# A state space stream with its dependent steps moved apart, the norm's roots at its end, and three small DMAs issued earlier

## The chip, the cores and the metric

The kernel runs on one core of one Trainium2 chip. The metric is device time in microseconds (us) of one execution, the median of several. TensorE (PE) multiplies, VectorE (DVE), ScalarE (ACT) and GpSimd (POOL) do the elementwise work, SyncE (SP) issues the weights' DMAs.

## The reference

Two blocks over 272 tokens (16 meta tokens and 256), width 1024. The first has layer norms, SwiGLU, a short convolution and a forgetting attention. The second, where the change is, has one mixer and one convolutional FFN. Of the mixer, this matters:

```python
u = rmsnorm(h, norm_w)
z, xbc, dt_raw, q, k, v, g_ssd, g_att = split_cols(u @ w_in, IN_WIDTHS)
xbc = silu(causal_dwconv(xbc, conv_w, conv_b))             # 4 taps
xs, bm, cm = split_cols(xbc, (2048, 512, 512))
dt = softplus(dt_raw + dt_bias) * valid
cs = cumsum(dt * a)
# 32 heads of 64, 8 heads share one of 4 groups of B and C:
lmat = exp(where(causal, cs[l] - cs[s], -inf))
y = einsum(C @ B^T, lmat, xs * dt) + d_skip * xs
g = y * silu(z)                                            # gated_group_rmsnorm
g = g * rsqrt(mean(g * g over each of 4 groups of 512) + EPS) * ssd_norm_w
y_ssd = g @ w_ssd_branch
merged = sigmoid(g_ssd + gb0) * y_ssd + sigmoid(g_att + gb1) * y_att
h = h + merged @ w_out
```

## The kernel before

**Weights.** Every product with a weight is done in three matmuls of float32r: the weight is split into a high half `wh` (ScalarE, a rounded copy, `high`) and a low half `wl` (VectorE or, for pieces named in `P.pool`, GpSimd, `low` and `low_pool`), and TensorE adds high by high, low by high and high by low (`gemm`, L834 and L836). A group is 256 output columns and, for 1024 rows, one unit of weights: 1 MB, one DMA on SP's queue, 4 pieces, 48 matmuls. A unit is split three groups ahead, in four pieces spread over the group that runs. Two pairs of PSUM banks alternate between groups.

**Side work.** All other work of the attention, the norms and the stream is cut into steps, one generator for each engine (`pe_steps`, `act_steps`, `dve_steps`, `pool_steps`). `Plan` says after which matmul of which group the next step is taken: `queue(n)` makes n steps available, `rate` is how many are taken in a group, `drain` takes what is left. All engines take the same number of steps at the same points of the groups, each in its own instruction order; a step may be empty (a bare `yield`, `idle(n)`). What an engine waits for is told by semaphores alone, and an engine that waits holds up all that stands behind it.

**The stream.** The conv output xs comes in 8 groups `("xs", j)` of two 128-row chunks, c = 2j and 2j+1; each chunk is two heads, h = 2c and 2c+1. `conv4` (taps) puts a group into CY: ScalarE the first tap, VectorE the other three for both chunks. `act_conv_end` makes TH = tanh(CY/2), `dve_conv_end` CY = (TH+1)*CY. Then, for each c, in this order of steps: y of c-2 (`pe_ssd_y`, products of XDT and EX; `dve_ssd_y` writes YB, adding the skip; `pool_ssd_y` multiplies by ZS, silu of z); the transposes of CY (L767) to PS[6], which VectorE scales by dt into XDT; a step for each head, in which TensorE broadcasts the cumulative sums (CSH, CSL) to PS[4] or PS[5], VectorE (even head) or ScalarE (odd head, two Relu passes) makes the exponent's argument, ScalarE the Exp, GpSimd the product with CBM, C B^T masked. Four EX buffers hold two c. Pair j ran in the group after xs j, its conv end as its first step.

**The norm.** After y of each fourth chunk, `act_gn`, `dve_gn` and `pe_gn` did a whole group g in five steps: squares of four chunks into SY (L1068), VectorE's sum of two halves (L1680), TensorE's mean (L670, L671) into PS[6], Ln and Exp on ScalarE (`act_rstd`, L953 and L955), the scale of YB (L1685), the high halves YH (L1079) and the low halves YL (L1691). Ln and Exp stand in another table set than the one the stream's Exp and Tanh use, so each norm group loads two tables.

**Behind the stream** come the groups `("gs", j)`, 4 of 258 columns, over which the last steps run, and `("ys", j)`, two units each, which read YH and YL.

**Ahead of it**, at the start of the mixer, GpSimd's queue issues eight small DMAs (L2092 to L2100): sinks, four cuts of the bias strips (2.2 MB in all, B2, B1, B0), and `ssd_dt_bias`, `ssd_a_log`, `ssd_d` (semaphore s_d). ScalarE waits for the last three before the scaled copy DC (L1344), and behind that stand the splits of the next unit and ZD (L1348), which empties the PSUM bank of the group dt. Softplus and a cumulative sum in nine dependent VectorE steps (L1471) follow ZD, then its transposes (L729).

Of the kernel before, what the change touches and what calls it, by code (L numbers as in the profile page):

```python
# [13 lines left out]
T = 272  # L14
# [169 lines left out]
def build(nc, A, out, scratch, ctx):  # L184
# [103 lines left out]
    with ExitStack() as st:  # L288
# [6 lines left out]
        SY = sb(st, "SY", [128, 4, NV])  # L295
# [43 lines left out]
    s_gsq, s_gadd, s_gsum, s_gn, s_yh, s_yl = (sem(n) for n in ("gsq", "gadd", "gsum", "gn", "yh", "yl"))  # L339
    s_gs2, s_gsg, s_m1, s_m2 = sem("gs2"), sem("gsg"), sem("m1"), sem("m2")  # L340
# [126 lines left out]
    def ssd_steps(c):  # L467
        return 3 + (c > 1) + 5 * (c > 1 and (c - 2) % 4 == 3)
    P.credit, P.rate, P.pool = -1.0, 8, (2,)
    for j in range(8):  # L470
# [4 lines left out]
        P.queue(1 + ssd_steps(2 * j) + ssd_steps(2 * j + 1))  # L475
    P.queue(7)
# [188 lines left out]
    def pe_gn(e, g):  # L665

        yield
        e.wait_ge(s_gadd, g + 1)
        e.wait_ge(s_xd, min(16, 4 * g + 5))
        e.matmul(PS[6][:, 0:NV], mean5[:], SY[:, 0, :], start=True, stop=False)  # L670
        e.matmul(PS[6][:, 0:NV], mean5[:], SY[:, 1, :], start=False, stop=True).then_inc(s_gsum, 1)  # L671
        yield
        yield from idle(3)

    def pe_steps(e):
# [73 lines left out]
        yield  # L749
        for c in range(16):  # L750
            if c % 2 == 0:
                yield
            if c > 1:
                pe_ssd_y(e, c - 2)
                yield
                if (c - 2) % 4 == 3:
                    yield from pe_gn(e, (c - 2) // 4)
# [5 lines left out]
            if c > 4 and (c - 5) % 4 == 0:  # L763
                e.wait_ge(s_lnv, 8 + (c - 5) // 4)
# [4 lines left out]
            yield  # L769
            for h in (2 * c, 2 * c + 1):  # L770
# [12 lines left out]
        for c in (14, 15):  # L783
            pe_ssd_y(e, c)
            yield
        yield from pe_gn(e, 3)
# [276 lines left out]
    def act_gn(e, g):  # L1063

        e.wait_ge(s_yz, 4 * g + 4)
        if g:
            e.wait_ge(s_gsum, g)
        e.activation(SY[:], YB[:, 4 * g:4 * g + 4, :], ACT.Square).then_inc(s_gsq, 1)  # L1068
        yield
        yield  # L1070
        e.wait_ge(s_gsum, g + 1)
        if g:
            e.wait_ge(s_gn, g)
        act_rstd(e, PS[6][:, 0:NV], 1, NV, 7 + g)
        yield
        e.wait_ge(s_gn, g + 1)
        for k0 in (4 * g, 4 * g + 2):
            for k in (k0, k0 + 1):
                e.activation(YH[:, k, :], YB[:, k, :], ACT.Copy, scale=pc("ssd_norm_w_2", k)).then_inc(s_yh, 1)  # L1079
            yield  # L1080

    def act_steps(e):
# [65 lines left out]
        yield from idle(5)  # L1148
        for c in range(16):
            if c % 2 == 0:  # L1150
                act_conv_end(e, 4 + c // 2)
                yield
# [801 lines left out]
    def pool_steps(e):  # L1954
# [30 lines left out]
        for c in range(16):  # L1985
            if c % 2 == 0:
                yield
# [187 lines left out]
```

## Time and profile before

| | us |
|---|---|
| median of 3 runs | 1780.92 (1780.73 to 1780.99) |
| the profiled execution, its own time | 1781.4 |
| its span | 1779.6 |
| TensorE busy | 1665.9 (94%) |
| VectorE busy | 1021.5 (57%) |
| ScalarE busy | 931.1 (52%) |
| GpSimd busy | 211.3 (12%) |

A share of the span is a mean over stages with different limits: the projections of the FFNs run with TensorE hardly ever idle, and the two stages in which it stops are read by themselves below. "Busy" of TensorE says nothing about its clock: the granted clock is a column of its own. In the waits, a row says which engine waited at which line for which instruction of another engine.

### The profile page before, as it was taken

To read this page: it belongs to the slowest core of one execution; us is meant where nothing else is said; L and a number is where in the kernel's file an instruction comes from. 1 tells how busy PE (TensorE), PEld (TensorE's weight loads), DVE (VectorE), ACT (ScalarE), POOL (GpSimd) and SP (SyncE) were. 2 spreads that over 40 slices of the span, in tenths; PEclk is the share of its full clock that TensorE was granted. 3 is DMA by queue.
4 is the path that set the end of the run, shared out by engine and by line. 5 is a ranking of instruction groups with operands and counts; after the bars stand their busy time and mean duration, and the time that the engine had idled before them with its cause. 6 is when DMAs were issued, how large, how long until landed. Compare 5 with 4: busy or idle time off the path is not lost. (4 is left out here: it accounts for less than half of the span.)

```text
span 1779.6 us, 31457 instructions
## 1 busy us (share of the span) xinstructions
PE 1665.9 (94%) x12901; PEld 1597.4 (90%) x12901; DVE 1021.5 (57%) x2083; ACT 931.1 (52%) x2018; POOL 211.3 (12%) x224
## 2 busy tenths in 40 slices
PE   8999999999999999999899997799997669999998
PEld 7999989899997999998899996788987558999997
DVE  6555566655545655554565554545375655668862
ACT  5444454644436544465554434566755556456652
POOL 4000000000000000001000001255423332200000
PEclk9999999999999999999999998999998889999999
DMA  8555535355554555553356553533442114545551
GB/s 258 184 167 172 184 123 186 119 181 175 171 172 131 178 179 179 159 160 101 119 167 190 178 181 102 151 102 112 134 151 62 58 48 126 182 143 190 183 165 56
DMA packets 260207, 266.00 MB, mean 149 GB/s; under 512 B 4755, under 2 KB 259025, under 8 KB 260064
## 3 DMA queue, kind: packets, MB, share of 16 engines
q1 hardware_dynamic: 258528, 260.72, 46.5%
q0 software_dynamic: 1536, 3.28, 0.8%
q8 instruction: 102, 1.67, 0.4%
q14 instruction: 41, 0.34, 0.1%
HBM read 262.89 MB, written 1.09 MB: 148 GB/s over the span
## 5 line engine op out<-in xcount | busy, mean ns | idle before, releaser
L1708 DVE TENSOR_TENSOR wl<-raw,wh 128x512 fp32r<-128x512 f32 x925 | 608.4, 711 | 392.4 <-ACT wh L1199 384.8
L1199 ACT ACTIVATE wh<-raw 128x512 fp32r<-128x512 f32 (+1 forms) x989 | 550.2, 621 | 213.0 <-PE ps L834 212.2
L834 PE MATMUL ps<-XH,wh 128*128 128x272 f32 (+2 forms) x2264 | 584.1, 293 | 21.4 <-ACT ZD L1348 8.6
L836 PE MATMUL ps<-XH,wl 128*128 128x272 f32 (+2 forms) x2264 | 574.4, 289 | 0.0
L834 PEld LDWEIGHTS ps<-XH,wh 128*128 128x128 f32 x2264 | 435.6, 192 | 27.1 <-issue 14.7
L836 PEld LDWEIGHTS ps<-XH,wl 128*128 128x128 f32 x2264 | 436.9, 193 | 0.2
L834 PE MATMUL ps<-XL,wh 128*128 128x272 f32 (+2 forms) x2264 | 319.1, 290 | 0.3 <-DVE XL L1463 0.3
L834 PEld LDWEIGHTS ps<-XL,wh 128*128 128x128 f32 x2264 | 294.8, 191 | 7.0 <-DVE XL L1463 4.2
L834 PE MATMUL ps<-HH,wh 128*128 128x272 f32 (+1 forms) x704 | 173.1, 284 | 0.0
L836 PE MATMUL ps<-HH,wl 128*128 128x272 f32 (+1 forms) x704 | 173.1, 284 | 0.0
L834 PEld LDWEIGHTS ps<-HH,wh 128*128 128x128 f32 x704 | 132.5, 188 | 0.0
L836 PEld LDWEIGHTS ps<-HH,wl 128*128 128x128 f32 x704 | 132.4, 188 | 0.0
L834 PE MATMUL ps<-KXH,wh 128*128 128x256 f32 (+1 forms) x480 | 121.2, 291 | 2.3 <-ACT KXH L943 2.3
L836 PE MATMUL ps<-KXH,wl 128*128 128x256 f32 (+1 forms) x480 | 118.0, 284 | 0.0
L1239 ACT ACTIVATE HH<-SG 128x272 fp32r<-128x272 f32 (+1 forms) x88 | 33.7, 426 | 148.4 <-DVE SG L1725 148.4
L2032 POOL TENSOR_TENSOR wl<-raw,wh 128x512 fp32r<-128x512 f32 x64 | 86.1, 1350 | 158.9 <-ACT wh L1199 158.9
L834 PEld LDWEIGHTS ps<-KXH,wh 128*128 128x128 f32 x480 | 91.2, 190 | 7.0 <-issue 5.4
L834 PE MATMUL ps<-HL,wh 128*128 128x272 f32 (+1 forms) x704 | 93.6, 284 | 0.0
L836 PEld LDWEIGHTS ps<-KXH,wl 128*128 128x128 f32 x480 | 91.5, 191 | 0.1
L834 PEld LDWEIGHTS ps<-HL,wh 128*128 128x128 f32 x704 | 89.0, 188 | 0.0
L1234 ACT ACTIVATE SG<-ps 128x272 f32<-128x272 f32 (+1 forms) x88 | 29.7, 389 | 102.8 <-PE ps L834 102.7
L1725 DVE SCALAR_TENSOR_TENSOR SG<-SG,ps 128x272 f32<-128x272 f32 (+1 forms) x88 | 33.8, 426 | 82.0 <-PE ps L834 82.0
(376 smaller groups left out, 1991.0 us busy)
## 6 DMA issues: line engine op xcount, KB each, us to landing
raw<-in_ffn_wg SPq DMA_DIRECT2D x44, 1024.0 KB, 5.4
raw<-in_ffn_wu SPq DMA_DIRECT2D x44, 1024.0 KB, 5.4
raw<-in_w_in SPq DMA_DIRECT2D x33, 1024.0 KB, 5.3
raw<-in_ffn_wd SPq DMA_DIRECT2D x32, 1024.0 KB, 5.1
raw<-in_w_ffn_in SPq DMA_DIRECT2D x22, 1024.0 KB, 5.1
raw<-in_ffn_wd SPq DMA_DIRECT2D x16, 768.0 KB, 4.7
raw<-in_conv_w_in SPq DMA_DIRECT2D x12, 1024.0 KB, 5.1
raw<-in_kv_w SPq DMA_DIRECT2D x8, 1024.0 KB, 5.4
```

Source lines behind the costliest of these rows:

```text
L834: mm = e.matmul(o, hi[:, k, c], xk, start=u.first and part == 0 and k == 0, stop=u.last and end)
L836: e.matmul(o, lo[:, k, c], xk, start=False, stop=False)
L1199: e.activation(wh[u.n % NH][:, c], raw[u.n % NR][:, c], ACT.Copy).then_inc(s_hi, 1)
L1234: e.activation(sg[:, m, n0:T], PS[G.b0 + m][:, 0:T - n0], ACT.Silu).then_inc(s_sg, 1)
L1239: e.activation(HH[f][:, 2 * j + m, n0:T], sg[:, m, n0:T], ACT.Copy).then_inc(s_hh, 1)
L1708: e.tensor_tensor(wl[u.n % NR][:, c], raw[u.n % NR][:, c], wh[u.n % NH][:, c].bitcast(F32), ALU.subtract).then_inc(s_lo, 1)
L1725: e.scalar_tensor_tensor(out=sg[:, m, n0:T], in0=sg[:, m, n0:T], scalar=0.5, in1=PS[G.b0 + m][:, 0:T - n0], op0=ALU.mult, op1=ALU.mult).th ...
L2032: e.tensor_tensor(wl[u.n % NR][:, c], raw[u.n % NR][:, c], wh[u.n % NH][:, c].bitcast(F32), ALU.subtract).then_inc(s_lop, 1)
```

## The change

1. **Order of the stream.** Pair j runs one group later, in the group after xs j+1. The conv end of the next group is taken between the two chunks of a pair (after the first transposes for ScalarE, after the argument for VectorE) instead of directly ahead of its own transposes. In each c one step does both heads on ScalarE, in the order Relu, Relu (odd), Exp (even), Exp (odd), and both products on GpSimd.
2. **Norm.** Squares, sum and mean of group g are taken in three different c (6+4g, 7+4g, 8+4g) and the mean is copied to a new tile VS. Ln and Exp of groups 0 to 2 are done at once, over 774 columns, at the end; group 3's after its own mean. The scales and the halves of all four groups follow there.
3. **Tables.** The set loaded ahead of the BC groups is `exp_and_others` instead of `natural_log_exp_and_others`; that one is loaded at the stream's end.
4. **Plan.** Other counts of steps, and a rate of 12 instead of 11.5 in the gs groups.
5. **Small DMAs.** The three of s_d are issued ahead of the sinks and the strips.

```diff
     def ssd_steps(c):
-        return 3 + (c > 1) + 5 * (c > 1 and (c - 2) % 4 == 3)
+        return 3 + (c > 1) + 2 * (c % 2 == 0 and c < 14) + (c > 5 and (c - 6) % 4 < 3)
...
             P.credit, P.rate = -4.0, 11.5
-        P.queue(1 + ssd_steps(2 * j) + ssd_steps(2 * j + 1))
-    P.queue(7)
+            P.queue(2)
+        else:
+            P.queue(ssd_steps(2 * j - 2) + ssd_steps(2 * j - 1))
+    P.queue(ssd_steps(14) + ssd_steps(15) + 12)
+    P.rate = 12
...
     def pe_gn(e, g):
-        yield
         e.wait_ge(s_gadd, g + 1)
-        e.wait_ge(s_xd, min(16, 4 * g + 5))
+        e.wait_ge(s_xd, (9, 13, 16, 16)[g])
+        if g:
+            e.wait_ge(s_vs, g)
...
-            if c > 4 and (c - 5) % 4 == 0:
-                e.wait_ge(s_lnv, 8 + (c - 5) // 4)
+            if c in (9, 13):
+                e.wait_ge(s_vs, (c - 5) // 4)
...
+        if step == 2:
+            e.wait_ge(s_gsum, g + 1)
+            e.activation(VS[:, g, :], PS[6][:, 0:NV], ACT.Copy).then_inc(s_vs, 1)
+
+    def act_gn_root(e, g0, g1):
+        e.wait_ge(s_vs, g1)
+        e.activation(VS[:, g0:g1, :], VS[:, g0:g1, :], ACT.Ln, bias=cc[:, 1:2]).then_inc(s_gl, 1)
+        e.wait_ge(s_gl, 1 if g0 == 0 else 2)
+        e.activation(VS[:, g0:g1, :], VS[:, g0:g1, :], ACT.Exp, scale=-0.5).then_inc(s_gr, 1)
...
+            if c % 2 == 0 and c < 14:
+                act_conv_end(e, 5 + c // 2)
                 yield
-        yield from idle(2)
-        yield from act_gn(e, 3)
+            yield
+            h = 2 * c + 1
+            E = EX[h % 4]
...
+            e.wait_ge(s_e, c + 1)
+            e.activation(EX[(h - 1) % 4][:], EX[(h - 1) % 4][:], ACT.Exp).then_inc(s_ee, 1)
+            e.wait_ge(s_er, c + 1)
+            e.activation(E[:], E[:], ACT.Exp, scale=-1.0).then_inc(s_ee, 1)
...
+        act_gn(e, 2, 2)
+        yield
+        e.preload_act_table_set("natural_log_exp_and_others")
+        yield
+        act_gn_root(e, 0, 3)
+        yield
+        yield
+        act_gn(e, 3, 0)
+        yield
+        act_gn_high(e, 0)
...
-        e.preload_act_table_set("natural_log_exp_and_others")
+        e.preload_act_table_set("exp_and_others")
...
+        dve_ssd_y(e, 15)
+        yield
+        dve_gn_scale(e, 0)
+        yield
+        dve_gn_low(e, 0)
+        yield
+        dve_gn_scale(e, 1)
+        dve_gn_add(e, 3)
+        yield
+        dve_gn_low(e, 1)
...
+        dd = A["ssd_d_2"]
+        e.dma_start(DTB[:], A["ssd_dt_bias_2"].rearrange("l p -> p l")).then_inc(s_d, 16)
+        e.dma_start(AN[:], A["ssd_a_log_2"].rearrange("l p -> p l")).then_inc(s_d, 16)
+        e.dma_start(DC2[:], bass.AP(tensor=dd.tensor, offset=dd.offset, ap=[[0, 128], [1, 32]])).then_inc(s_d, 16)
         e.dma_start(SNK[:], bass.AP(tensor=sk.tensor, offset=sk.offset, ap=[[0, 128], [1, 16]])).then_inc(s_b, 16)
```

VectorE in the stream before, one projection group: after the taps (CY from PSUM) one split, then the conv product (CY from TH), and at once YB, XDT and the argument of the next chunk.

```order
L1766 SCALAR_TENSOR_TENSOR CY<-ps,PV,CY 128x269 x2
L1708 TENSOR_TENSOR wl<-raw,wh 128x512
L1675 SCALAR_TENSOR_TENSOR CY<-TH,CY 128x272 x2
L1708 TENSOR_TENSOR wl<-raw,wh 128x512
L1699 SCALAR_TENSOR_TENSOR YB<-CY,DC,ps 128x258
L1649 TENSOR_TENSOR XDT<-ps,DTT 128x256
L1651 TENSOR_TENSOR XDT<-ps,DTT 16x128
L1661 TENSOR_SCALAR EX<-ps,NCT 128x272
L1662 TENSOR_SCALAR EX<-ps,NCT 128x144
```

And after the change, the same place, here with a norm group's sum (SY) in it:

```order
L1829 SCALAR_TENSOR_TENSOR CY<-ps,PV,CY 128x269 x2
L1771 TENSOR_TENSOR wl<-raw,wh 128x512
L1744 TENSOR_TENSOR SY<-SY 128x516
L1762 SCALAR_TENSOR_TENSOR YB<-CY,DC,ps 128x258
L1771 TENSOR_TENSOR wl<-raw,wh 128x512
L1686 TENSOR_TENSOR XDT<-ps,DTT 128x256
L1688 TENSOR_TENSOR XDT<-ps,DTT 16x128
L1699 TENSOR_SCALAR EX<-ps,NCT 128x272
L1700 TENSOR_SCALAR EX<-ps,NCT 128x144
L1739 SCALAR_TENSOR_TENSOR CY<-TH,CY 128x272 x2
```

The conv product (CY from TH) moved from ahead of XDT to behind the first chunk's argument: it now serves the pair that follows.

VectorE at the end of the stream after the change, from y of chunk 15 on (scale: YB from VS; low halves: YL):

```order
L1762 SCALAR_TENSOR_TENSOR YB<-CY,DC,ps 128x258
L1771 TENSOR_TENSOR wl<-raw,wh 128x512
L1749 TENSOR_TENSOR YB<-YB,VS 128x1032
L1755 SCALAR_TENSOR_TENSOR YL<-YB,PV,YH 128x258 x4
L1749 TENSOR_TENSOR YB<-YB,VS 128x1032
L1744 TENSOR_TENSOR SY<-SY 128x516
L1755 SCALAR_TENSOR_TENSOR YL<-YB,PV,YH 128x258 x4
```

The sum of the last norm group's squares (SY) stands behind the scale and low halves of group 0 and the scale of group 1.

## Rows read from the trace of the kernel before

**Rows 1.** Windows: length, busy PE PEld DVE ACT POOL, clock, DMA share, GB/s.
```profile
1328.50:1498.40 169.90, 123.22 (x849) 109.32 (x848) 97.88 (x201) 91.37 (x182) 60.80 (x60) 0.85 0.22 69
```

**Rows 2.** Waits, 1320 to 1500 us: total us, times, longest us.
```profile
PE ps L767 <- DVE CY L1675: 30.5, 8, 6.9
...
PE ps L670 <- DVE SY L1680: 13.9, 4, 4.5
```

**Rows 3.** Timeline of TensorE from 1409 us: start us, length, what [idle before].
```profile
1409.50 1.16 PE L670 MATMUL ps<-SY,mean 128*128 128x258 f32 x2 [4.47 <-DVE SY L1680]
...
1410.96 3.05 PE L834 MATMUL ps<-XL,wh 128*128 128x272 f32 x14
...
1414.22 0.29 PE L836 MATMUL ps<-XH,wl 128*128 128x272 f32 x1
...
1414.81 0.29 PE L836 MATMUL ps<-XH,wl 128*128 128x272 f32 x1
...
1417.07 0.29 PE L836 MATMUL ps<-XH,wl 128*128 128x272 f32 x1
...
1418.59 0.29 PE L836 MATMUL ps<-XH,wl 128*128 128x272 f32 x1
```

**Rows 4.** Timeline of TensorE from 1123 us, a run of 16 matmuls.
```profile
1128.65 2.17 PE L834 MATMUL ps<-XL,wh 128*128 128x272 f32 x16
```

**Rows 5.** Timeline of TensorE from 1474 us: first matmuls of gs 3 and ys 0.
```profile
1492.77 0.28 PE L834 MATMUL ps<-XH,wh 128*128 128x258 f32 x1
...
1498.53 0.28 PE L834 MATMUL ps<-YH,wh 128*128 128x258 f32 x1
```

**Rows 6.** Groups by line, 1330 to 1490 us: count, busy us, mean ns, idle.
```profile
L1997 POOL TENSOR_TENSOR EX<-EX,CBM 128x416 f32<-128x416 f32 x32 | 34.3, 1072 | 70.3 <-ACT EX L1171 63.6 <-ACT EX L1168 6.7
...
L1708 DVE TENSOR_TENSOR wl<-raw,wh 128x512 fp32r<-128x512 f32 x28 | 24.3, 871 | 17.6 <-ACT wh L1199 17.6
...
L1675 DVE SCALAR_TENSOR_TENSOR CY<-TH,CY 128x272 f32<-128x272 f32 x16 | 8.2, 555 | 1.2 <-ACT TH L1061 1.2
```

**Rows 7.** DMA issues from 1100 to 1130 us: KB each, us to landing.
```profile
SNK<-in_attn_sinks POOLq DMA_DIRECT2D x1, 8.0 KB, 2.9
...
DC<-in_ssd_d POOLq DMA_DIRECT2D x1, 16.0 KB, 12.7
```

**Rows 8.** Timelines of ScalarE and TensorE from 1100 us, two waits and the transposes.
```profile
1119.45 0.45 ACT L1344 ACTIVATE DC<-DC 64x16 f32<-64x16 f32 x2 [14.45 <-DMA DC<-in_ssd_d]
...
1123.10 0.60 PE L834 MATMUL ps<-XH,wh 128*128 128x272 f32 x1 [8.56 <-ACT ZD L1348]
...
1136.81 0.21 PE L729 MATMUL ps<-ident,ZD 32*128 32x32 f32 x1 [0.98 <-issue]
```

**Rows 9.** Timeline of VectorE from 1350 us: the taps of one group.
```profile
1358.14 2.60 DVE L1766 SCALAR_TENSOR_TENSOR CY<-ps,PV,CY 128x271 f32<-128x271 f32 x6 [0.54 <-ACT CY L1253]
```

**Rows 10.** The page's groups, whole kernel: the splits on VectorE.
```profile
L1708 DVE TENSOR_TENSOR wl<-raw,wh 128x512 fp32r<-128x512 f32 x925 | 608.4, 711 | 392.4 <-ACT wh L1199 384.8
```

**Rows 11.** Timeline of ScalarE from 1326 us: squares and a root's table load.
```profile
1369.49 1.06 ACT L1068 ACTIVATE SY<-YB 128x1032 f32<-128x1032 f32 x1 [2.38 <-POOL YB L2024]
...
1373.29 1.28 ACT L955 ACT_TABLE_LOAD   x1
```

**Rows 12.** Timeline of VectorE from 1350 us: a scale, four low halves.
```profile
1375.04 1.23 DVE L1685 TENSOR_TENSOR YB<-YB,RS 128x1032 f32<-128x1032 f32 x1 [3.15 <-ACT RS L955]
...
1376.85 1.70 DVE L1691 SCALAR_TENSOR_TENSOR YL<-YB,PV,YH 128x258 fp32r<-128x258 f32 x4 [0.58 <-ACT YH L1079]
```

**Rows 13.** Instructions on the tile raw, the window 1103 to 1104: unit z 0.
```profile
L2144 SPq DMA_DIRECT2D raw<-in_w_in x1: 368/368/368, 1103.5 to 1103.5; - x1
...
DMA to landing us min/median/max: 17.2/17.2/17.2
```

**Rows 14.** Timeline of VectorE from 1119 us: first split of z 0, last sum.
```profile
1127.39 0.69 DVE L1708 TENSOR_TENSOR wl<-raw,wh 128x512 fp32r<-128x512 f32 x1
...
1136.29 0.42 DVE L1471 TENSOR_TENSOR CSB<-CSB 32x272 f32<-32x272 f32 x1
```

More of the change, by code:

```diff
@@ L749, in pe_steps @@
         yield
+        yield from idle(2)
         for c in range(16):
-            if c % 2 == 0:
-                yield
             if c > 1:
@@ L769, in pe_steps @@
             yield
+            yield from idle(c % 2 == 0 and c < 14)
             for h in (2 * c, 2 * c + 1):
@@ L782, in pe_steps @@
                 yield
[L783 to L786, printed above, removed]
+            yield from idle(c % 2 == 0 and c < 14)
+            if c > 5 and (c - 6) % 4 < 3:
+                if (c - 6) % 4 == 2:
+                    pe_gn(e, (c - 6) // 4)
+                yield
+        pe_gn(e, 2)
+        yield
+        pe_ssd_y(e, 14)
+        yield
+        yield
+        pe_ssd_y(e, 15)
+        yield
+        yield from idle(3)
+        pe_gn(e, 3)
+        yield
+        yield from idle(4)
         for j in range(4):
@@ new lines, in act_steps @@
+            e.wait_ge(s_e, c + 1)
[3 more added lines that the diff above has]
+            yield
+            yield from idle(c % 2 == 0 and c < 14)
+            if c > 5 and (c - 6) % 4 < 3:
+                act_gn(e, (c - 6) // 4, (c - 6) % 4)
+                yield
+        act_gn(e, 2, 2)
+        yield
+        e.preload_act_table_set("natural_log_exp_and_others")
@@ L1655, in dve_steps @@
             yield
+            yield from idle(c % 2 == 0 and c < 14)
             h = 2 * c
@@ L1928, in vector @@
         side.run(at["out2"])
-        norm(11, UT2, 8, TS, "norm_ffn_w_2", 64)
+        norm(7, UT2, 8, TS, "norm_ffn_w_2", 64)
         for j in range(11):
@@ L1984, in pool_steps @@
         yield
+        yield from idle(2)
         for c in range(16):
-            if c % 2 == 0:
-                yield
             if c > 1:
@@ L1990, in pool_steps @@
                 yield
-                if (c - 2) % 4 == 3:
-                    yield from idle(5)
+            yield
+            yield from idle(c % 2 == 0 and c < 14)
             yield
@@ L1997, in pool_steps @@
                 e.tensor_tensor(E[:], E[:], CBM[:, g, 0:416], ALU.mult).then_inc(s_em, 1)
-                yield
-        for c in (14, 15):
-            pool_ssd_y(e, c)
             yield
-        yield from idle(5 + 4)
+            yield from idle((c % 2 == 0 and c < 14) + (c > 5 and (c - 6) % 4 < 3))
+        yield
+        pool_ssd_y(e, 14)
+        yield
+        yield
+        pool_ssd_y(e, 15)
+        yield
+        yield from idle(8 + 4)
         for k in range(KD):
```

142 lines of the change are left out of this document (73 added, 69 removed).

## The prediction

> **What bounds the kernel now.** I read the groups of instructions first: TensorE is busy 94% of the span, so time is lost only where it stops or runs at its lower clock. The waits, cut to one stage after the other, show two such places.
>
> The first is the state space stream, from the end of the projection group xs 0 (1328.5 us) to the first matmul on YH (1498.4 us), 169.9 us. TensorE is busy 123.2 us of them at a mean granted clock of 0.85 [rows 1]. The waits name the idle 46.7 us: 30.5 us in 8 waits of the transposes of CY for VectorE's half of the convolution's end, 13.9 us in 4 waits of the norm's mean for VectorE's sum of squares [rows 2]. Each long wait has a tail: after the 4.47 us wait at 1409.5 the matmuls of about 0.21 us (14 from 1410.96 on, 3.05 us) are those of the lower level of the clock, 1.2 GHz [rows 3].
>
> What would the stage take with no wait at 2.4 GHz? A projection matmul of 272 columns takes (2.17 - 0.29) / 15 = 0.125 us [rows 4], a group of 48 takes 6.03 us; a group of 258 columns takes 1498.53 - 1492.77 = 5.76 us [rows 5]. Seven xs groups and four gs groups: 42.2 + 23.0 = 65.2 us. One step c of the stream adds its transposes (1414.22 to 1414.81, less two matmuls: 0.34 us), four broadcasts at 0.125 (0.50 us) and the y products (1417.07 to 1418.59, less two matmuls: 1.27 us) [rows 3]: 2.11 us, 16 times, 33.8 us. Four norm means cost 1409.50 to 1410.96 = 1.5 us at half clock, about 0.85 at full: 3.4 us. The floor is 102.4 us, so 67.5 us of the stage are loss: 46.7 us idle and 20.8 us of slow clock.
>
> The second place is at 1114.5 us. ScalarE waits for a small table (ssd_d) until 1119.45, 14.45 us, TensorE 8.56 us behind it [rows 8]. ssd_d took 12.7 us to land because it was issued behind the bias strips; the sinks table, issued ahead of them, took 2.9 us [rows 7]. After the stall TensorE runs at the lower level for 3.1 us, the first matmul taking 0.60 us [rows 8]: about 1.5 us more.
>
> **The stream, part by part.** The work of TensorE is the same, 538 projection matmuls from the last BC product to YH in both orders; only positions change. Before, a pair of steps c ran in the group after its projection: 12 matmuls and one y product after that group's end its transposes came, while ScalarE and VectorE still had to do the taps (2.60 us on VectorE after ScalarE's first tap [rows 9]), the tanh and the product. Now the pair runs one group later and its convolution end is half a group before its first transposes. For xs 1: projection ends, taps done about 3.2 us later, tanh at 3.9, product by about 7.0 where VectorE has a scale step in front of it; the transposes come 60 matmuls and two steps' other work (1.7 us) after, at 9.2 us. Eight waits, 30.5 us, go.
>
> What is late next? In the steady part TensorE needs 6.03 + 4.22 = 10.25 us for a pair. I followed VectorE in the new order from a projection's end: taps to 3.2 us, split, YB 4.2, split, XDT 5.4, exponent argument 6.2, conv product 7.0, YB 7.4, XDT 8.05, split, argument 9.4 (with 0.48 for a YB, 0.42 + 0.27 for XDT and 0.49 + 0.35 for an argument, the means of the groups by line). TensorE asks for YB at 5.85, XDT at 7.2, the argument at 7.95: about 1.7 us of cover each. The y products of c need two GpSimd products of 1.07 us [rows 6]; they are done about 3 us before. This exchange of ScalarE's Relu and Exp costs nothing at that cover; without it each c would pay.
>
> VectorE is nearly full, though. Its 97.9 us in this stage [rows 1] are nearly unchanged in content against a floor of 102.4. Part of them is stretching: the 28 splits took 871 ns on average here against 711 over the whole kernel, and the 16 conv products 555 ns against an undisturbed 430 or so, 28 x 0.16 + 16 x 0.125 = 6.5 us [rows 6, 10]. GpSimd's 60.8 us come closer together in a stage of 113 us, so I take half as much again, 3 us, and 1 us for the start of the stream, where two steps stand close: **4 us** of new stall together (bounds 0 and 20 us, rival 1).
>
> The rule behind that is the Trainium skill's, page "SBUF — State Buffer", section "Who interferes with whom": a VectorE instruction with two SBUF inputs and a GpSimd instruction that reads SBUF exclude one another for the whole instruction. It speaks against packing this stage tighter. The taps, which read one input from PSUM, show no such stretching here (493 ns on average, 487 least), so the trace agrees.
>
> **The norm.** For groups 0 to 2 the squares, the sum, the mean and a copy to VS are a step c apart (5 us), so their three waits in the stream go. The mean of group 2 comes where c = 15 is dense: squares at ScalarE after its exponentials, VectorE's sum behind a split: 0.8 us late. All roots go to the end: 8 table loads of 1.28 us [rows 11] leave ScalarE, one is added, and the first load of the stream too goes, since the set that is loaded ahead now holds tanh. ScalarE was not what TensorE waited for, so I count that at nothing.
>
> The Trainium skill's page "ScalarE: Activation LUTs", section "What ACT_TABLE_LOAD costs", has about 2.66 us for a switch with its drain; here the Exp follows its load at once, so the row's 1.28 us decides. By either figure TensorE's sum stays as it is, as ScalarE has slack.
>
> The last mean pays for this. From the end of y 15: root of groups 0 to 2 ready at about +1.1 us (copy, load, two takes of GS, a split, Ln and Exp over 774 columns); VectorE then does a whole scale of group 0 (1.23 us), four low halves (1.70 us) that wait for ScalarE's high halves, which stand behind the squares of group 3 (1.06 us) [rows 11, 12], and the scale of group 1, before it sums group 3's squares. That ends at about +6.4 us; TensorE gets there at +1.9: **4.5 us** of stall, and 1.6 us of slow clock after it, as at 1409.5. Behind it stand 72 matmuls, 8.6 us; ScalarE's last high halves are needed only in the second unit of the first ys group, 6 us later still. They are ready at about +15 us, so ys starts on time.
>
> Stage: 102.4 + 4 + 0.8 + 4.5 + 1.6 = 113.3 us, against 169.9: **56.6 us less**.
>
> **The small DMAs.** Moved ahead of five others, three issues of 0.53 us: the strips start 1.7 us later. Their first reader stands behind four more projection groups, so that costs nothing. ssd_d lands about 2.9 us after its issue, by 1105.5, where ScalarE gets to it. TensorE passes 1114.5 without its 8.56 us. What is late next is a weight load: unit z 0, issued at 1103.5, took 17.2 us [rows 13] beside the strips, to 1120.7. VectorE's first split of it was at 1127.39 before, and its cumulative sums, in order behind it, ended at 1136.71, 9.3 us later [rows 14]; TensorE's transposes that need them came at 1136.81 [rows 8]. Now the split can start at 1121.4, the sums end at 1130.7, and TensorE, there by 1125.5, stops for 5 us. The rest of the kernel moves by 6.0 us; the new stop is long enough to lower the clock, 1.5 us. **4.5 us less.** Bounds: 3.2 if the strips hold z 0 back by another 1.3 us, 7.5 if the weights, with a head start, land 1.5 us earlier and the clock holds.
>
> **The sum.** The profiled execution took 1781.4 us with a span of 1779.6, 0.5 us above the median of 1780.92. 1781.4 - 56.6 - 4.5 = 1720.3; against the median 1719.8. I say **1720 us**.
>
> **The rivals.**
> 1. VectorE becomes the bound. For: 98 us of work in 102. If each of five two-input instructions of a pair waits for half a GpSimd product (0.55 us) instead of 0.17, a pair costs 1.9 us more on VectorE, over eight pairs 15 us. Against: margins of 1.7 us take up part. **1735 us.**
> 2. The convolution's end is not early enough, since each engine takes it in order behind other steps. If half of the 30.5 us stays (at other instructions perhaps) with half of the clock's loss, 15 + 10 us: **1745 us.**
> 3. Slower than before: GpSimd's pair of products reaches TensorE too late in every step c. ScalarE now starts Relu before it has VectorE's argument and does both Exp behind it. It decides from 3 us of lateness on, my cover; each microsecond more costs 16. To eat 60 us the chain of two products (2.1 us) and three ScalarE passes would have to come 6.8 us later than I have it. The rows show GpSimd idle for 70.3 us ahead of these products, waiting for ScalarE's Exp [rows 6], which speaks for the mechanism, and TensorE never waiting for the products, which speaks against it. A new lateness of 7 us: **1784 us.**
> 4. The order doesn't do what it says. The instruction rows above show that it does: no separate chance.
>
> **How the numbers follow.** Forecast 0.62, rival 1 0.22, rival 2 0.13, rival 3 0.03. The forecast's own bounds are 1710 (no new stall from packing, the clock kept twice, 7.5 us from the DMAs) and 1730; with rival 1 and its neighbourhood to 1743 the range holds more than 8 in 10: **1710 to 1743**. A measurement tells 0.2%, 3.6 us, from no change. Faster by more: 0.96; within: 0.01; slower: 0.03.
>
> **What would show it.** In the profile of the changed kernel: no wait of the CY transposes for the conv product over 1 us; mean waits of groups 0 and 1 at zero and one wait of 4 to 5 us before the last; granted clock 1.00 from the third xs group to the second gs group; the wait for ssd_d gone and TensorE idle about 5 us before the transposes of ZD; stage near 113 us; splits in it at 0.9 to 1.0 us. It is wrong if pairs take over 11.5 us each, or if TensorE waits for YB or XDT in each step.

## The result and the profile after

The changed kernel takes **1731.55 us** (median of four; 1726.82 to 1734.70) against 1780.83 for the kernel before: ratio 0.9722, 95% interval 0.9699 to 0.9745. That is 49.3 us less, where I had forecast 61 less and 1720; the time lies inside the range. The kernel before kept within 1 us in these four runs (within 3 to 4 us over nine runs in each later measurement), the changed one spread over 8 us, and that needs an explanation of its own.

The profiled execution is the 1734.70 one, span 1732.9. The same stretch as in [rows 1], from the end of xs 0 to the first matmul on YH; columns: stretch, length, busy time and count of PE, PEld, DVE, ACT and POOL, granted clock, DMA share, GB/s. The second row is all that follows it:

```profile
1324.20:1451.70 127.50, 111.01 (x851) 97.90 (x850) 100.56 (x200) 80.90 (x175) 68.19 (x60) 0.92 0.29 92
...
1452.00:1732.90 280.90, 267.88 (x2203) 265.73 (x2202) 184.54 (x352) 155.37 (x314) 17.12 (x15) 0.98 0.48 154
```

The stage fell from 169.9 to 127.5 us: 42.4 less, forecast 56.6 less. TensorE is idle 16.5 us of it (46.7 before); 127.5 - 16.5 - 102.4 leaves 8.6 us of slow clock (20.8 before). Behind YH nothing changed: 281.2 us to the span's end, as before. What TensorE waited for in the stage (us in total, times, longest), against [rows 2]:

```profile
PE ps L675 <- DVE SY L1744: 10.0, 2, 6.2
PE ps L675 <- DVE XDT L1688: 3.4, 1, 3.4
PE ps L675 <- issue: 1.9, 1, 1.9
PE ps L664 <- DVE YB L1762: 0.9, 2, 0.7
PE ps L781 <- DVE EX L1700: 0.2, 1, 0.2
```

The eight waits of the CY transposes (30.5 us) are gone, and nearly nothing stands in the steps themselves. All that is left, 15.3 us, is L675: the four means of the norm, 3.4, 1.9, 3.8 and 6.2 us. Here are the first and the last of them with what VectorE did ahead of each (start, length, instruction, idle before it and what ended it); first group 0:

```profile
1374.74 2.59 DVE L1829 SCALAR_TENSOR_TENSOR CY<-ps,PV,CY 128x271 f32<-128x271 f32 x6 [1.52 <-ACT CY L1292]
1377.25 0.68 DVE L1771 TENSOR_TENSOR wl<-raw,wh 128x512 fp32r<-128x512 f32 x1
1377.85 0.69 DVE L1744 TENSOR_TENSOR SY<-SY 128x516 f32<-128x516 f32 x1
1378.46 0.47 DVE L1762 SCALAR_TENSOR_TENSOR YB<-CY,DC,ps 128x258 f32<-128x258 f32 x1
1378.85 0.68 DVE L1771 TENSOR_TENSOR wl<-raw,wh 128x512 fp32r<-128x512 f32 x1
1379.45 0.41 DVE L1686 TENSOR_TENSOR XDT<-ps,DTT 128x256 f32<-128x256 f32 x1
1379.79 0.27 DVE L1688 TENSOR_TENSOR XDT<-ps,DTT 16x128 f32<-16x128 f32 x1
...
1380.20 1.20 PE L675 MATMUL ps<-SY,mean 128*128 128x258 f32 x2 [3.41 <-DVE XDT L1688]
```

The mean writes the PSUM bank in which the transposes of CY lie, so it must wait until XDT of step 8 has read them, and VectorE does that XDT behind the taps of the next projection group, 2.59 us, and four other instructions. I had called these waits zero because the sum of squares would be ready. TensorE asks at 1376.8; the sum is there at 1378.5 and the bank at 1380.1, so of the 3.4 us the sum accounts for the first 1.7 and the bank for the rest. For group 1 (asked at 1404.1, sum at 1404.4, bank at 1405.9) nearly all is the bank. Group 3:

```profile
1434.30 1.23 DVE L1749 TENSOR_TENSOR YB<-YB,VS 128x1032 f32<-128x1032 f32 x1
1436.10 1.69 DVE L1755 SCALAR_TENSOR_TENSOR YL<-YB,PV,YH 128x258 fp32r<-128x258 f32 x4 [0.58 <-ACT YH L1096]
1437.70 1.23 DVE L1749 TENSOR_TENSOR YB<-YB,VS 128x1032 f32<-128x1032 f32 x1
1438.85 1.76 DVE L1744 TENSOR_TENSOR SY<-SY 128x516 f32<-128x516 f32 x1
...
1440.66 1.23 PE L675 MATMUL ps<-SY,mean 128*128 128x258 f32 x2 [6.19 <-DVE SY L1744]
```

This is the stall that I forecast, scale, low halves, scale, sum, with 4.5 us; it took 6.2, the sum alone 1.76 us where an undisturbed one takes 0.69. Each of the four stops has slow matmuls behind it: the mean's own two took 1.20 and 1.23 us in these rows. At group 2, whose stop was 3.8 us, they still took 0.70, and the granted clock fell right behind them, to 0.50 in the window from 1428 to 1430.

In the other stretch, that of the small tables, ScalarE no longer waits for ssd_d, and TensorE's wait of 8.56 us [rows 8] is gone. The stop that I had forecast ahead of the transposes of ZD is there, and so is the unit of weights that ScalarE waits for:

```profile
1125.57 1.67 ACT L1238 ACTIVATE wh<-raw 128x512 fp32r<-128x512 f32 x3 [4.49 <-DMA raw<-in_w_in]
...
1129.87 0.28 PE L732 MATMUL ps<-ident,ZD 32*128 32x32 f32 x1 [4.37 <-issue]
```

Sliding window attention starts at 1142.3 instead of 1146.5: 4.2 us gained, forecast 4.5.

### The profile page after: what moved, and what is told of

The parts are those of the page before. It is cut to its first block, busy times and chain, and to the rows that moved or that the text cites. A ratio compares the mean times of both kernels' runs of the same rounds, so it can differ in the third digit from the quotient of the medians.

```text
span 1732.9 us, 31446 instructions
## 1 busy us (share of the span) xinstructions
PE 1654.6 (95%) x12901; PEld 1585.6 (91%) x12901; DVE 1025.5 (59%) x2083; ACT 918.3 (53%) x2010; POOL 219.2 (13%) x224
## 4 chain that ended last, share of the span: by engine, by line
PE 87%; DVE 6%; ACT 5%; issue 2%; DMA 0%; SPq 0%; DVEq 0%; ACTq 0%
PE ps L847 53%; PE ps L849 25%; PE ps L531 1%; DVE wl L1771 1%; ACT wh L1238 1%; DVE CY L1829 1%; ACT XH L956 1%; PE ps L816 1%; PE ps L630 1%; ACT H L961 1%; DVE CY L1739 0%; PE ps L631 0%; PE ps L664 0%; PE ps L619 0%; ACT swP L987 0%
## 5 line engine op out<-in xcount | busy, mean ns | idle before, releaser
L847 PE MATMUL ps<-XH,wh 128*128 128x272 f32 (+2 forms) x2264 | 578.1, 291 | 12.8 <-ACT XH L956 6.7
L849 PEld LDWEIGHTS ps<-XH,wl 128*128 128x128 f32 x2264 | 432.5, 191 | 0.2
```

Source lines behind the costliest of these rows:

```text
L847: mm = e.matmul(o, hi[:, k, c], xk, start=u.first and part == 0 and k == 0, stop=u.last and end)
L849: e.matmul(o, lo[:, k, c], xk, start=False, stop=False)
```

## The experiments

Twelve runs. Times are medians of four or five; the stage runs from the end of xs 0 to the first matmul on YH in the profiled execution, and swa is the start of sliding window attention in it, at which all that comes ahead has been paid.

| kernel | us (lowest to highest) | ratio to before, 95% | swa | stage | TensorE idle in it | clock |
|---|---|---|---|---|---|---|
| before | 1779.4 to 1780.8 (medians) | 1 | 1146.5 | 169.9 | 46.7 | 0.85 |
| changed | 1731.6 (1726.8 to 1734.7) | 0.9699 to 0.9745 | 1142.3 | 127.5 | 16.5 | 0.92 |
| again | 1726.7 (1726.3 to 1730.8) | 0.9698 to 0.9725 | 1136.7 | 124.8 | 16.4 | 0.95 |
| dma_back | 1736.8 (1736.3 to 1738.7) | 0.9748 to 0.9775 | 1148.1 | 125.9 | 16.5 | 0.93 |
| sum3_first | 1726.3 (1725.8 to 1728.9) | 0.9690 to 0.9717 | 1136.8 | 122.8 | 15.8 | 0.96 |
| means_later | 1728.1 (1722.7 to 1729.8) | 0.9691 to 0.9720 | 1142.4 | 121.1 | 14.1 | 0.96 |
| strips_later | 1734.3 (1726.3 to 1734.9) | 0.9710 to 0.9747 | 1141.8 | 127.7 | 16.4 | 0.92 |
| strips_wait | 1727.4 (1725.3 to 1728.5) | 0.9690 to 0.9716 | 1137.1 | 126.5 | 16.4 | 0.93 |
| vector_splits | 1732.0 (1729.2 to 1736.0) | 0.9713 to 0.9739 | 1143.3 | 128.0 | 16.7 | 0.92 |
| short_products | 1723.2 (1723.1 to 1730.5) | 0.9675 to 0.9709 | 1136.9 | 121.3 | 13.0 | 0.94 |
| exp_order | 1739.7 (1739.4 to 1744.5) | 0.9762 to 0.9789 | 1137.0 | 137.2 | 23.2 | 0.90 |
| before_exchange | 1772.9 (1771.9 to 1773.6) | 0.9948 to 0.9973 | 1145.5 | 162.4 | 39.9 | 0.86 |
| best | 1716.8 (1716.1 to 1722.5) | 0.9634 to 0.9662 | 1143.4 | 114.4 | 8.7 | 0.99 |
| best2 | 1718.4 (1717.0 to 1719.1) | 0.9641 to 0.9667 | 1136.8 | 115.4 | 9.4 | 0.99 |

**The changed kernel again.**

> The changed kernel once more, five rounds, to know its spread, since its first four times lay 8 us apart (1726.8 to 1734.7) where the kernel before kept within 1 us. If the spread comes from stops of 3 to 6 us before the norm's means, behind which TensorE falls to 1.2 GHz for a phase that differs from run to run, the times again lie between 1726 and 1735. If it was the chip of that call, they lie within 2 us.

Three of five at 1726.3 to 1726.7, two at 1728.9 and 1730.8; with the first four, four times near 1726.5 and five between 1729 and 1735. The two profiles (1734.7 and 1726.3) say where such runs part, first at a place ahead of everything the diff touches. A norm makes TensorE stop for 6.2 us until 1087 in both, and its matmuls behind that stop run at half clock in both. The clock is back by 1093, then TensorE stops again, for 2.2 us, for the high half of the normed activations (XH). In the 1734.7 run, then in this one:

```profile
1086.00:1092.00 6.00, 5.12 (x11) 3.87 (x12) 0.00 (x0) 2.65 (x5) 0.00 (x0) 0.50 0.00 0
1092.00:1094.00 2.00, 1.38 (x6) 0.81 (x4) 0.00 (x0) 0.55 (x2) 0.00 (x0) 0.97 0.00 0
1094.00:1098.00 4.00, 2.39 (x10) 2.42 (x11) 3.53 (x10) 3.42 (x9) 0.00 (x0) 0.69 0.00 0
```
```profile
1086.00:1092.00 6.00, 5.67 (x15) 4.43 (x16) 0.00 (x0) 2.13 (x4) 0.00 (x0) 0.59 0.00 0
1092.00:1094.00 2.00, 0.49 (x3) 0.06 (x1) 0.42 (x2) 0.92 (x2) 0.00 (x0) 1.00 0.00 0
1094.00:1098.00 4.00, 3.28 (x26) 3.31 (x27) 4.00 (x12) 3.95 (x10) 0.00 (x0) 1.00 0.00 0
```

Behind the stop of 2.2 us the clock falls a second time in the first run, until 1098.9, and holds in this one. Why it does so is not shown. From there it is the DMAs: the release of a weight buffer lets SyncE issue unit z 0 at 1103.4 in the one and at 1101.0 in the other, GpSimd's strips (2.2 MB) start at 1103.2 and 1102.3, and unit z 1, issued at 1108.5 and 1109.1, stands behind them. Issues of that moment (KB, us to landing), first and second run:

```profile
raw<-in_w_in SPq DMA_DIRECT2D x1, 1024.0 KB, 17.1
```
```profile
raw<-in_w_in SPq DMA_DIRECT2D x1, 1024.0 KB, 11.5
```

z 1 lands at 1125.6 or at 1120.6. ScalarE wants it at 1121.1 in the first run and at 1122.7 in the second, so only the first one stops, and loses 5.6 us by the start of sliding window attention. All nine profiled runs that have the new DMA order and do not make the strips wait for z 1 fall on one of these two courses: the clock held behind the 2.2 us in four (again, sum3_first, short_products, exp_order), whose attention starts at 1136.7 to 1137.0, and fell in five (changed, means_later, strips_later, vector_splits, best), where it starts at 1141.8 to 1143.4.

The clock parts the runs once more: this run's stage is 2.7 us shorter at the same idle time, clock 0.95 against 0.92. The first matmuls of the mean of group 1 show where, behind a stop of the same length in both, first and second run:

```profile
1405.98 1.05 PE L675 MATMUL ps<-SY,mean 128*128 128x258 f32 x2 [1.93 <-issue]
```
```profile
1399.33 0.67 PE L675 MATMUL ps<-SY,mean 128*128 128x258 f32 x2 [1.94 <-issue]
```

**The DMA order undone.**

```
         e.dma_start(B0[:], shifted(...)).then_inc(s_b, 16)
+        (dt_bias, a_log, ssd_d again here, behind the sinks and strips)
```

> The changed kernel with the three small loads (dt_bias, a_log, ssd_d) again behind the sinks, the strips and their pieces; the stream stays as changed. Theory: this part alone is worth 4.2 us, the gain read at the first matmul of the sliding window attention (1146.5 before, 1142.3 after), so 1735 to 1737 us, with ScalarE's wait of 14 us for ssd_d and TensorE's 8.6 us back and the 4.4 us before the transposes of ZD gone. Rival: what TensorE gains there is given back, since a later stop moves the clock's low phase, and the time stays within 2 us of the changed kernel's.

1736.8 us: the part is worth about 5 us against the slower course (1731.5) and 10 against the faster one (1726.7). Theory held for the first; I had no term for the second. With the table behind the strips TensorE stops for 9.5 us, until 1124.6 in the profiled run, and all four times lie within 2.4 us. In this order the stop takes up the difference between the courses: before_exchange below, with the old order, is on the fast course, and its attention starts only 1.0 us ahead of the kernel before, which is on the slow one. The change took away the stop that hid the fork.

**The strips later.**

```
-        (four strips issues)
         group("kv2")
         group("dt")
+        group(("q2", 0))
+        (four strips issues)
```

> The changed kernel, with GpSimd's four issues of the strips (2.2 MB) moved from before the group kv2 to behind the group q2 0, some 16 us later. Theory: the changed kernel has two ways through this place. Where TensorE's clock recovers late from the norm before it, weight unit z 1 is issued at 1108.4 beside the strips and lands after 17.1 us, ScalarE waits 4.5 us for it and TensorE 4.4 us with a slow clock behind; where the clock recovers early, it lands after 11.5 us and nothing waits, and the run is 5 us shorter. With the strips out of its way z 1 lands after 6 to 9 us in every run, and all runs lie near the lower value: 1724 to 1728 us, with sliding window attention starting at or before 1137. Rival: the strips now land behind 1137, and VectorE's first sum with them waits: 1730 us or more. Second rival, the strips aren't the cause: the runs again lie in two groups 5 us apart.

This missed its aim. GpSimd has no split in these groups, so its next instruction is still the issue: nothing moved in time, and z 1 took 16.1 us. The run is one more of the changed kernel, 1734.2 to 1734.9 three times and 1726.3 once. The second attempt makes GpSimd wait for z 1:

```
+        z1 = groups["z", 1].units[0].n
+        e.wait_ge(s_raw[z1 % NR], 16 * (z1 // NR + 1))
         (four strips issues)
```

> The changed kernel, with GpSimd waiting for the landing of weight unit z 1 before it issues the strips; the run before this one had moved the issues only past groups in which GpSimd has no work, so the strips still went out at the same time. Theory: z 1 is issued at 1108.4 and, with only z 0 beside it, lands after 5 to 7 us instead of 17.1 (late clock) or 11.5 (early clock). TensorE's wait of 4.4 us before the transposes of ZD and the half clock behind it go, and the two groups of times that the changed kernel shows (1726.5 and 1731.5) close to one: 1723 to 1727. The strips then land by about 1130, ahead of VectorE's first use at 1137. Rival: the strips come too late for that use, or z 2 and z 3 beside them do, 1730 us or more. Second rival: nothing to do with the strips, two groups again.

The strips go out at 1114.7, and z 1, issued at 1109, has landed by then:

```profile
raw<-in_w_in SPq DMA_DIRECT2D x1, 1024.0 KB, 5.3
```

and TensorE's wait ahead of the transposes of ZD is

```profile
1127.35 0.21 PE L732 MATMUL ps<-ident,ZD 32*128 32x32 f32 x1 [1.22 <-issue]
```

The stop fell from 4.4 to 1.2 us, sliding window attention starts at 1137.1 though the clock fell a second time here, and five runs lie within 3.2 us. The strips beside z 1 were what turned the clock's 3 us into the gap of 5.6 us. The repair removes the slower course and gives nothing against the faster one: 1727.4 us against 1726.7.

**The last sum first.**

```
+        dve_gn_add(e, 3)
         dve_gn_scale(e, 0)
...
         dve_gn_scale(e, 1)
-        dve_gn_add(e, 3)
```

> The changed kernel, but VectorE sums the squares of group 3 before it scales group 0, where it stood behind the scale of 0, the low halves of 0 and the scale of 1. Theory: TensorE asks for the last mean at 1434.3 and ScalarE's squares of group 3 end at 1434.8, so the sum ends at 1435.6 and the wait of 6.2 us falls to 1.3 us; with the slow matmuls behind it (about 2 us) 6 to 7 us less than the changed kernel, 1724 to 1726 us. The high and low halves come 0.7 us later and hide. Rival: VectorE is full, and the wait comes back before the first YH matmul: same time as the changed kernel.

1726.3 us, the same as the changed kernel again (1726.7): the stage is 2.0 us shorter, what follows it 2.0 us longer. The wait fell as expected, 6.2 to 1.2 us, and 4.3 us of it came back at the first YH matmul:

```profile
1440.79 0.64 ACT L1262 ACTIVATE GS<-ps 128x258 f32<-128x258 f32 x2
...
1441.52 0.55 PE L847 MATMUL ps<-YH,wh 128*128 128x258 f32 x1 [4.29 <-ACT GS L1262]
```

The rival was right in its result, though what the trace shows is a chain and not VectorE's load. From the first scale to the last high half VectorE and ScalarE pass the four groups to and fro, scale 1.23, high 0.6 until the first low, four lows 1.69: 3.5 us a group, 14 us in a chain, and ScalarE's take of the last GS, which frees the bank that YH needs, stands behind the last high halves. The stall of 6.2 us had covered that chain. The new stop's slow clock falls behind the first YH matmul, which is the 2.0 us: the 56.5 us from there on, in the changed kernel again and here,

```profile
1443.46:1500.00 56.54, 56.07 (x465) 55.76 (x464) 37.84 (x58) 31.83 (x61) 13.30 (x10) 1.00 0.56 187
```
```profile
1441.52:1498.06 56.54, 56.54 (x455) 56.54 (x456) 37.15 (x57) 32.54 (x63) 13.76 (x10) 0.96 0.48 158
```

**The first two means later.**

```
-    (c > 5 and (c - 6) % 4 < 3)          squares, sum, mean in c = 6, 7, 8 and 10, 11, 12
+    (c in NORM)                          in c = 7, 8, 9 and 11, 12, 13; group 2 unchanged
```

> The changed kernel, but squares, sum and mean of groups 0 and 1 each one step c later (7, 8, 9 and 11, 12, 13 for 6, 7, 8 and 10, 11, 12), so that the mean stands behind the XDT of an odd step, which no taps precede on VectorE. Theory: the waits of 3.4 us at 1380 and 1.9 us at 1406 are for XDT of step 8 and 12, which VectorE does behind the taps of the next group; both go, with the slow clock behind them (1.5 to 3 us): 6 to 8 us less, 1723 to 1726 us. Rival, VectorE full: the same 5 us come back as waits of y products or broadcasts, and the time stays within 2 us of the changed kernel's.

Partly. The stage is 121.1 us, 3.7 to 6.4 less, but the waits only fell from 3.4 and 1.9 to 2.7 and 0.8 us, and 2.0 us came back at the y products, which now wait 2.9 us for YB instead of 0.9. The time, 1728.1 us, can't be told from the changed kernel's 1731.6 and 1726.7. VectorE is still behind at the odd step: from the start of the taps it works without a gap for 11 us (1376.3 to 1387.6 in the trace of best).

**What GpSimd's accesses cost.**

```
-                e.tensor_tensor(E[:], E[:], CBM[:, g, 0:416], ALU.mult)
+                e.tensor_tensor(E[:, 0:32], E[:, 0:32], CBM[:, g, 0:32], ALU.mult)
```

> The changed kernel, but GpSimd multiplies only 32 of the 416 columns of each exponential by C-B (32 products of 1.20 us become short; the rest of the product is left out). It measures what GpSimd's accesses cost VectorE. Theory, contention: VectorE's pair of convolution products, 2.2 us where it meets them, falls to 0.9; the sums for the norm from 1.2 and 1.6 to 0.7; the splits from 0.81 to 0.7; so XDT and the sums end 1 to 2 us earlier, the waits before the means of groups 0 and 1 fall from 3.4 and 1.9 us to under 2 together, and the stage from 126 to 129 us to 120 to 122. The wait of 6.2 us before the last mean stays at 5.5 or more, since it is VectorE's order and not its speed. Rival, order alone: the waits of groups 0 and 1 stay over 4 us together and the stage within 2 us.

VectorE's convolution products over the stage (busy, mean ns), changed kernel and this one:

```profile
L1739 DVE SCALAR_TENSOR_TENSOR CY<-TH,CY 128x272 f32<-128x272 f32 x16 | 14.9, 972 | 0.0
```
```profile
L1739 DVE SCALAR_TENSOR_TENSOR CY<-TH,CY 128x272 f32<-128x272 f32 x16 | 10.0, 662 | 0.0
```

So the stretching is real, 555 ns before the change [rows 6], 972 after, 662 without the long products. Against the changed kernel again TensorE's idle time fell by 3.4 us, the stage by 3.5 to 121.3 and the time by 3.5; the first three means wait 2.7, 1.4 and 2.6 us, the last still 6.1. The long products account for a sixth of what the four means wait (15.1 to 12.8 us). GpSimd's splits and its part of y are still there, so a sixth is the least that contention costs; that all the rest is order is not shown. The expected fall to under 2 us together for the first two did not come (4.1).

**More work for VectorE.**

```
-    P.credit, P.rate, P.pool = -1.0, 8, (2,)
+    P.credit, P.rate, P.pool = -1.0, 8, ()
```

> The changed kernel, but VectorE also does the weight splits that GpSimd does in the stream, 11 of 1.37 us on GpSimd, some 0.7 to 0.8 us each on VectorE. It asks whether VectorE is the bound of the stream (my rival 1). If it is, its 8 to 9 us more come out whole, less what GpSimd's 15 us of fewer accesses give back in stretching (2 to 4 us): 4 to 7 us slower than the changed kernel, with new waits of TensorE at y products and broadcasts. If it has slack outside the places before the means, only the two longest waits grow: within 2 us of the changed kernel (1726 to 1732).

1732.0 us. The times can't tell (1729.2 to 1736.0 against 1726.3 to 1734.9 for strips_later beside it); the stage can, 128.0 against 127.5 at the same clock. In the stage VectorE did eight more instructions and GpSimd eight fewer, and VectorE's busy time fell from 100.6 to 97.0 us, since without GpSimd's splits the convolution products took

```profile
L1739 DVE SCALAR_TENSOR_TENSOR CY<-TH,CY 128x272 f32<-128x272 f32 x16 | 7.1, 480 | 0.0
```

7.8 us less than in the changed kernel, more than the splits cost. VectorE's pair of products and then, from GpSimd's timeline, what ran beside it, changed kernel and this one:

```profile
1356.96 2.25 DVE L1739 SCALAR_TENSOR_TENSOR CY<-TH,CY 128x272 f32<-128x272 f32 x2
...
1356.38 1.28 POOL L2098 TENSOR_TENSOR wl<-raw,wh 128x512 fp32r<-128x512 f32 x1
1357.69 2.48 POOL L2059 TENSOR_TENSOR EX<-EX,CBM 128x416 f32<-128x416 f32 x2
```
```profile
1360.68 0.77 DVE L1739 SCALAR_TENSOR_TENSOR CY<-TH,CY 128x272 f32<-128x272 f32 x2
...
1360.82 3.11 POOL L2059 TENSOR_TENSOR EX<-EX,CBM 128x416 f32<-128x416 f32 x2 [1.26 <-ACT EX L1184]
```

Where GpSimd is already at work VectorE's pair takes 2.25 us; where VectorE starts first it takes 0.77 and GpSimd's pair takes 3.11 instead of 2.48. The loss did not go away, it moved to the engine that has time. Because VectorE's busy time fell, this run did not load it harder; what it shows is that 3.6 us less on VectorE do not shorten the stage. That VectorE isn't the bound of the steady part shows in the changed kernel itself: TensorE's groups from 1338.6, 1348.8 and 1359.3 on take 10.2, 10.5 and 11.1 us, with 0.9 us of waits in all, against 10.25 for its own work.

**ScalarE's order in a step.**

```
-            (Relu, Relu of the odd head) (Exp even) (Exp odd)
+            (Exp even) (Relu, Relu of the odd head) (Exp odd)
```

> The changed kernel with ScalarE's order inside a step c as before: Exp of the even head (which waits for VectorE's argument), then the two Relu and the Exp of the odd head; nothing else. My prediction said that without the exchange each c would pay. In the trace of the changed kernel ScalarE's Relus (0.49 and 0.37 us) lie in its wait of 1.4 us for the argument; behind the Exp they make the odd head's Exp 0.9 us later. If each c pays this: 10 to 14 us slower, near 1740 us, with waits of y products for GpSimd's product. If the cover of some 3 us that GpSimd's products had in my sum is real, the exchange is worth nothing: within 2 us of the changed kernel.

1739.7 us, stage 137.2 against 124.8 at the same swa start: 12.4 us. It is not paid at GpSimd's products, nor in each c. VectorE's taps of two successive groups, first in the changed kernel, then here:

```profile
1351.65 2.58 DVE L1829 SCALAR_TENSOR_TENSOR CY<-ps,PV,CY 128x271 f32<-128x271 f32 x6 [1.52 <-ACT CY L1292]
1362.94 2.59 DVE L1829 SCALAR_TENSOR_TENSOR CY<-ps,PV,CY 128x271 f32<-128x271 f32 x6 [1.52 <-ACT CY L1292]
```
```profile
1348.38 2.59 DVE L1829 SCALAR_TENSOR_TENSOR CY<-ps,PV,CY 128x271 f32<-128x271 f32 x6 [2.31 <-ACT CY L1292]
1360.47 2.59 DVE L1829 SCALAR_TENSOR_TENSOR CY<-ps,PV,CY 128x271 f32<-128x271 f32 x6 [2.32 <-ACT CY L1292]
```

ScalarE makes the first tap, right behind the exponentials. With the Relus behind the first Exp it comes 0.8 us later, VectorE waits 2.3 instead of 1.5 us and all that follows in the pair shifts: 12.1 us a pair instead of 11.3. TensorE now waits 1.4 us for YB in two pairs (0.2 and 0.7 before), and the first three means wait 4.8, 3.5 and 5.1 us: 6.8 us of idle time and 5.6 of slow clock. The cost goes by the tap, for which I had computed no cover.

The exchange alone on the kernel before:

> The kernel before with the exchange alone: ScalarE does the Relus of the odd head ahead of both Exp, all in the odd head's step. In the changed kernel undoing this cost 10 to 12 us. Theory: it is worth that only once the steps are packed; in the kernel before TensorE stands 30.5 us at transposes of CY behind the whole chain taps, tanh, product, and finds the exponentials done, so the time stays within 2 us of the kernel before. Rival: the exchange is worth the same by itself, since ScalarE's tanh and squares come 0.9 us earlier in each c: 8 to 12 us less than before.

1772.9 us, 7 us less (ratio 0.9960, interval 0.9948 to 0.9973). I was wrong, and the rival, with 8 to 12 us, was near. The row of [rows 2] reads there:

```profile
PE ps L767 <- DVE CY L1675: 22.7, 8, 4.8
```

7.8 us less over the eight waits, but unevenly: three hardly change, the others are 0.8 to 2.4 us shorter. In the second pair VectorE's wait for the first tap fell from 2.3 to 1.5 us and TensorE's from 4.2 to 3.4, so there the gain begins at the first tap; for the larger ones that is not shown.

**All repairs.**

```
+        (means one step later; strips moved as in strips_later)
+        dve_gn_add(e, 2) directly behind the argument of c = 15, ahead of the split
-        scale 0 | low 0 | scale 1, sum 3 | low 1 | scale 2 | low 2 | scale 3 | low 3
+        scale 0, sum 3 | scale 1 | low 0 | scale 2 | low 1 | scale 3 | low 2 | low 3
```

> The changed kernel with all four repairs: strips later; means of groups 0 and 1 one step later; group 2's sum directly behind the last argument, ahead of the split; at the end VectorE takes scale 0, then the sum of group 3, and each scale one ahead of its low halves. Theory: in the run with the means later the stage from the last B-C product to the first matmul on YH took 122.6 us (changed kernel: 126.3 and 129.0). The waits of 6.4 and 1.2 us before the last two means fall to 1.2 and 0.3, and the chain of scales and halves, 3.5 us a group when each waits for the other engine, falls to 3 us a group, so that it no longer holds back the last take of GS as it did when the sum of group 3 alone was put first (4.3 us wait): stage 114 to 117 us, time 1713 to 1719 us. Rival, VectorE full: the stage stays at 120 us or more, with waits at y products and broadcasts, and the time at 1720 us or more.

**1716.8 us**, the best of the study, 13 us under the changed kernel by the ratios (0.9648 and 0.9722), 11 under its second measurement (0.9712). Stage 114.4 us, clock 0.99; the wait of group 2 is gone, that of group 3 is 1.9 us, and YH waits 0.2 us for GS. Stage and time are as expected. What is left of TensorE's waits:

```profile
PE ps L666 <- DVE YB L1766: 2.8, 3, 1.7
PE ps L677 <- DVE XDT L1690: 2.6, 1, 2.6
PE ps L677 <- DVE SY L1748: 1.9, 1, 1.9
PE ps L677 <- issue: 0.8, 1, 0.8
```

Its strips are not really later either (z 1 took 17.3 us), so one variant more:

```
+        strips wait for z 1
+        mean of groups 0 and 1 directly ahead of the y products of c = 8 and 12
```

> The version with all repairs (1716.8), with the strips now really later (GpSimd waits for z 1), and the means of groups 0 and 1 one slot later still, directly ahead of the y products of c = 8 and 12, because TensorE still waited 2.6 and 0.8 us for XDT of the odd step there. Theory: both waits fall to under 1 us together (XDT ends 2.6 us after TensorE asks, of which the slot gives back about 1 to 1.5 us and the y products, which wait there anyway, the rest), the clock stays at its upper level, and the late landing of z 1 goes: stage 111 to 114 us, time 1709 to 1714 us. Rival: the copy of the mean by ScalarE, for which the next transposes wait, takes the place of the wait: stage as before, 115 us or more, time 1714 or more.

1718.4 us, not faster. The strips did their part (z 1 in 5.2 us, swa at 1136.8, 6.6 us earlier than in best's profile), but the stage, 115.4 us, did not profit from the later slot: 2.2 and 0.9 us of wait at the means, 0.8 us at the transposes for ScalarE's copy of them. Best's profiled run was its longest (1722.5), on the slower course; its other three lie at 1716.1 to 1716.9. If they took the faster course, as seems likely though no trace shows it, there was nothing for the strips to gain, as in strips_wait, and the stage's 1.0 us more is what is left.

## Why the prediction was right, and where it was short

- **Bound, floor and place of the loss**: right. The floor of 102.4 us stands: in the stretch 1340 to 1375 the changed kernel's TensorE works at full clock with about 1 us of idle time, and its groups take what the sum says once their waits are taken off.
- **The convolution's ends, 30.5 us, gone**: right, no wait of the transposes is left. Rival 2 did not occur. Not all of it is the work of the later pairs, though: the exchange of ScalarE's passes alone took the 30.5 us to 22.7 on the kernel before. No run undoes the order of the pairs or that of the norm by itself, so their shares are read from the waits.
- **The packing, 4 us**: too high, 1.2 us (YB and an argument). The stretching itself is larger than I took (972 ns, not 0.68 us, for the convolution product), but VectorE has the cover. Rival 1 did not occur: the groups named under vector_splits take 10.2 to 11.1 us, where it asked for some 12, and hardly wait.
- **Means of groups 0 and 1 "go"**: wrong, 5.3 us. The step that failed is "a step c apart, so their waits go". I looked for who makes the mean's input and not for who frees its bank; VectorE does both behind the taps of the next group. The bank accounts for 3.2 us of the two waits and the sum, late as well, for 2.1.
- **Mean of group 2, 0.8 us**: mis-sized, 3.8. A split that waited 2.2 us for ScalarE's high half stood ahead of the sum, and the sum took 1.55 us. In best, with the sum ahead of the split, the wait is gone.
- **Last mean, 4.5 us**: mechanism right, size 6.2: the stretched sum (1.76 us) and, by the order of the rows, the scales start later behind the late mean of group 2.
- **Slow clock, 1.6 us**: mis-sized, 8.6, or 6.0 in the second profile. I priced one stop; there were four, each with its tail. In the faster course the 1.9 us stop cost no clock. Together, for the first profile: 10.0 more at the means, 2.8 less from packing, 7.0 more of slow clock make the 14.2 us between 113.3 and 127.5.
- **Table loads at nothing**: not tried by itself; no wait of TensorE in the stage has a load ahead of it.
- **The small DMAs, 4.5 us**: 4.2 in the profiled run. The unit that comes late is z 1 and not z 0: z 0, issued beside the strips' start, landed in 8.1 us instead of the 17.2 of [rows 13]. That the forecast fits is partly luck, and it holds for one of two courses; in the other the part is worth 10 us, above my bound of 7.5.
- **The exchange costs nothing, and without it each c would pay**: right that it matters, but unpriced and for another reason (the first tap, and not GpSimd's products in each c): undone, it takes back 12.4 of the 45.1 us that the stream gained in that comparison; alone, it gives 7.
- **Signs named ahead**: the CY waits, ssd_d and the stop before ZD came as said; the mean waits and clock 1.00 from the third xs group to the second gs group did not. The splits took 0.80 us here, not 0.9 to 1.0. As for the Trainium skill's page "SBUF — State Buffer", section "Who interferes with whom", the trace agrees in kind: VectorE's two-input products stretch beside GpSimd's splits and products (972 ns on average, 662 with GpSimd's products short, 480 where VectorE started first), the taps at 0.43 us each do not.

## What to carry to other kernels

When a step is moved away from the work it waited for, ask of each of its instructions two things: who makes its input and by when, and who frees the buffer or bank that it writes. Price a stop with its slow clock behind it, as often as there are stops; here 15.3 us of waits brought up to 8.6 more. A stall that is taken away uncovers the chain behind it, so cost the next chain before you count the gain.

## What the chip showed that I had not expected

Behind the same short stop, one program had TensorE's clock held at 2.4 GHz in one run and at half of it for 3 us in another: behind 2.2 us ahead of the small tables, and again behind 1.9 us in the stream. Where the first of these came, one weight unit was issued 2.4 us later, and the next unit, queued with 2.2 MB of strips, landed in 17.1 us instead of 11.5: 5.6 us in the end. Making the strips wait closed that gap. So a forecast to 0.3% for such a kernel has to name its course. And eight splits handed from GpSimd to VectorE added nothing to VectorE's busy time, since its convolution products fell from 972 to 480 ns while GpSimd's own rose from 1199 to 1291.
